# Four small SBUF tiles moved from ahead of the weight ring to behind it

## The reference

```python
mod = silu(c) @ w_ada + b_ada             # 2048 -> 6 * 2048: sh1, sc1, gt1, sh2, sc2, gt2
h = rms_norm(x, g_pre_mix) * (1 + sc1) + sh1
u_lru, u_gate, q, k, v, f = split(h @ w_in)          # 2048 -> 5 * 1024 + 8
y_lru = rg_lru(conv4(u_lru)) * gelu(u_gate)          # 16 blocks of 64, scan over the tokens
y_att = causal attention, 8 heads of 128, bias from cumsum(log_sigmoid(f + b_forget))
y = concat(rms_norm(y_lru), rms_norm(y_att)) @ w_out # 2048 -> 2048
x = x + gt1 * rms_norm(y, g_post_mix)
h = rms_norm(x, g_pre_mlp) * (1 + sc2) + sh2
y = square(relu(h @ w_ff1)) @ w_ff2                  # 2048 -> 8192 -> 2048
x = x + gt2 * rms_norm(y, g_post_mlp)
```

## Time and profile before

| | |
|---|---|
| median of 3 runs | 2133.91 us (2131.73 to 2133.93) |
| the profiled execution | 2131.73 us, of which its span, first to last instruction, is 2129.9 us |
| mean granted TensorE clock | 0.990 of full speed |
| TensorE busy | 2052.9 us, 96% of the span |
| VectorE, ScalarE, GpSimd busy | 1614.7, 797.4 and 99.2 us |
| HBM read and written | 313.20 and 10.52 MB |

### The profile page before, as it was taken

The page is one execution under the profiler, slowest core; times in us unless marked ns, Lnnn a source line. Parts: engine busy times, 40 slices in busy tenths (PEclk is TensorE's granted clock), DMA queues, the critical chain, the costliest instruction groups (busy, mean ns, idle before and its releaser), DMA issues.

```text
span 2129.9 us, 25152 instructions
## 1 busy us (share of the span) xinstructions
PE 2052.9 (96%) x9025; PEld 1673.3 (79%) x9025; DVE 1614.7 (76%) x1863; ACT 797.4 (37%) x1035; POOL 99.2 (5%) x105
## 2 busy tenths in 40 slices
PE   4999999999999999999999999999999999999997
PEld 4777778788778778888888888888888888888886
DVE  6998597876987887686776776876866867767766
ACT  5324622214553254343343343333333433433433
POOL 1001050000220001000000000000000000000000
PEclk8999999999999999999999999999999999999999
DMA  9995459856437862332332332333223323333334
GB/s 330 364 302 173 148 159 306 288 183 210 129 108 274 271 237 83 125 99 89 108 98 91 117 106 90 108 99 108 95 85 125 98 89 108 98 94 120 102 120 157
DMA packets 181582, 324.57 MB, mean 152 GB/s; under 512 B 12648, under 2 KB 49624, under 8 KB 179216
## 3 DMA queue, kind: packets, MB, share of 16 engines
q1 hardware_dynamic: 173600, 302.08, 43.9%
q0 software_dynamic: 3568, 16.95, 2.2%
q10 hardware_dynamic: 4352, 4.73, 0.7%
HBM read 313.20 MB, written 10.52 MB: 152 GB/s over the span
## 4 chain that ended last, share of the span: by engine, by line
PE 77%; DVE 14%; DMA 3%; issue 3%; ACT 3%; SPq 1%; DVEq 0%; ACTq 0%
PE pair L835 10%; PE pair L837 10%; PE pair L836 10%; PE pair L860 9%; PE pair L862 9%; PE pair L861 9%; PE bank L527 4%; PE bank L528 4%; PE bank L529 4%; DVE acc L1443 2%; DVE w_lo L1415 2%; PE bank L537 2%; PE bank L539 1%; PE bank L538 1%; DMA raw<-in_w_out_dram 1%
## 5 line engine op out<-in xcount | busy, mean ns | idle before, releaser
L1863 DVE TENSOR_TENSOR yg<-yg,pair 128x1024 f32<-128x1024 f32 x240 | 289.6, 1217 | 287.6 <-PE pair L862 287.5
L835 PE MATMUL pair<-h_hi,w_lo 128*128 128x512 f32 x1020 | 397.5, 390 | 0.0
L836 PE MATMUL pair<-h_lo,w_hi 128*128 128x512 f32 x1020 | 396.9, 389 | 0.0
L837 PE MATMUL pair<-h_hi,w_hi 128*128 128x512 f32 x1020 | 396.8, 389 | 0.0
L860 PE MATMUL pair<-w_hi,op_lo 128*128 128x512 f32 x840 | 329.9, 393 | 9.1 <-DVE op_lo L1830 8.6
L861 PE MATMUL pair<-w_lo,op_hi 128*128 128x512 f32 x840 | 327.2, 389 | 0.0
L862 PE MATMUL pair<-w_hi,op_hi 128*128 128x512 f32 x840 | 327.1, 389 | 0.0
L965 ACT ACTIVATE w_hi<-raw 128x1024 fp32r<-128x1024 f32 (+1 forms) x114 | 118.6, 1044 | 317.2 <-DMA raw<-in_w_in_dram 205.3
L835 PEld LDWEIGHTS pair<-h_hi,w_lo 128*128 128x128 f32 x1020 | 191.5, 188 | 39.9 <-issue 0.2
L836 PEld LDWEIGHTS pair<-h_lo,w_hi 128*128 128x128 f32 x1020 | 191.4, 188 | 39.9 <-issue 0.2
L837 PEld LDWEIGHTS pair<-h_hi,w_hi 128*128 128x128 f32 x1020 | 191.5, 188 | 39.9
(11 more groups left out here) (272 smaller groups left out, 2773.4 us busy)
## 6 DMA issues: line engine op xcount, KB each, us to landing
raw<-in_w_ada_dram SPq DMA_DIRECT2D x128, 512.0 KB, 4.7
w_raw<-in_w_ff_dram SPq DMA_DIRECT2D x128, 512.0 KB, 3.9
raw<-in_w_ff_dram SPq DMA_DIRECT2D x128, 512.0 KB, 4.6
raw<-in_w_in_dram SPq DMA_DIRECT2D x74, 512.0 KB, 4.8
gst<-in_w_ada_dram SPq DMA_DIRECT2D x64, 512.0 KB, 9.3
raw<-in_w_out_dram SPq DMA_DIRECT2D x32, 512.0 KB, 4.8
x_tok<-in_x_dram SPq DMA_DIRECT2D x4, 1024.0 KB, 8.6
xr<-in_x_dram POOLq DMA_DIRECT2D x4, 1024.0 KB, 7.8
```

Source lines behind the costliest of these rows:

```text
L835: pe.matmul(b, lo[:, cols], h_hi[:, kt, :], start=(kt == 0), stop=False)
L836: pe.matmul(b, hi[:, cols], h_lo[:, kt, :], start=False, stop=False)
L837: last = pe.matmul(b, hi[:, cols], h_hi[:, kt, :], start=False, stop=(kt == KT - 1))
L1863: dve.tensor_tensor(y, y, pairs[2 + (i + r) % 2][:, :, :], ALU.subtract if i == 6 else ALU.add).then_inc(product_read, 1)
```

## The change

The four tiles `bf`, `eps`, `mod` and `A1` are no longer allocated first. `A1` stands ahead of `S1`, and the other three behind `wf_raw`, as the last of the tiles that live through the whole kernel. No instruction, wait, DMA, loop or shape is changed.

```diff
-        bf = sb("bf", [HEADS, 1])
-        eps = sb("eps", [P, 1])
-        mod = sb("mod", [P, 4])
-        A1 = sb("A1", [P, KT])
         raw = sb("raw", [P, RING, 2 * COLS])
         w_hi = sb("w_hi", [P, RING, 2 * COLS], F32R)
         w_lo = sb("w_lo", [P, RING, 2 * COLS], F32R)
...
         cc = sb("cc", [P, 4, KT])
-        S1, A2, S2 = (sb(n, [P, KT]) for n in ("S1", "A2", "S2"))
+        A1, S1, A2, S2 = (sb(n, [P, KT]) for n in ("A1", "S1", "A2", "S2"))
         stat = sb("stat", [P, 96])
         lam = sb("lam", [P, 8, CT])
         wf_raw = sb("wf_raw", [P, KT, HEADS])
+        bf = sb("bf", [HEADS, 1])
+        eps = sb("eps", [P, 1])
+        mod = sb("mod", [P, 4])
```

## The result

The changed kernel takes 2169.35 us (median of 4 runs, 2168.16 to 2171.3), the kernel before 2133.8 us in the same session. The ratio is 1.0167, with a 95% interval of 1.0154 to 1.0178: it is slower by 35.6 us. The forecast was 2133.9 us with a range up to 2162.0. The result is outside the range and on the side that had a chance of 0.32.

The account below looks back on a forecast made before the run. The prediction took TensorE to bound the kernel (96% busy). It added 0 for every term to the profiled 2131.7 us, giving 2133.9 us as a median, with a range of 2111 to 2162 us.

Parts of the forecast that it names:

- What bounds the kernel: Whole kernel: TensorE busy 96% of the span, 77% of the chain; matmul cost changes come out almost one to one.
- VectorE, ScalarE, the moved tiles: 0: Operations on shifted tiles and few short uses of the four moved ones: 0, bound 2.4 us either way.
- DMA: 0, with 6.6 us either way: Loads written into raw, 43.7 us of the chain: 0, bounded by a 15% landing difference, 6.6 us.
- The rule on 256-byte boundaries: DMA writes into raw: 2048 bytes would need 68 beats instead of 65, some 2 us; left out of the sum.
- TensorE, the ring as streamed operand: 0: 3864 matmuls streaming the weight tiles, no cover, about 3500 counting fully: 0 taken, -35 to +23 us possible.
- one piece of 64 bytes: Streamed matmuls: one more 64-byte piece per misplaced run, 16 cycles or 6.7 ns each, 23 us either way.
- TensorE, the ring as stationary operand: 0, covered: 4608 matmuls loading the weight tiles: 0, since up to 39 ns more per load hides behind the matmul streaming beside it.
- The sum: Whole kernel: profiled 2131.7 us plus 0 for every term gives 2131.7, or 2133.9 us as a median.
- (b): Start distance in product and w1_piece: weight tiles and activations out of step, slower, 2157 or 2188 us; chance 0.28.
- (a): Matmuls streaming the weight tiles: faster from a multiple of 64, 2111 to 2099 us; chance 0.18.
- (c): Loads of raw slower or faster by up to 6.6 us, 2127 to 2140.5; chances 0.03 small, 0.02 faster, 0.04 slower.
- The 16-byte lines: SBUF lines of 16 bytes: all starts before and after are multiples of 32, so nothing would change.

Follow-up runs that it names:

- m2_fine: Layer left out, TensorE alone: float32r at fine distances, plain float32, bfloat16 and 256 columns; float32r of 512 columns settles between 226.7 and 240.0 ns.
- e1: Kernel before with one more 32-byte tile at the front, so weight tiles and activations both move up by 32: 2131.77 us, ratio 0.9999.
- m1_map: Also called the map: layer left out, TensorE alone, float32r matmuls at 256 pairs of start addresses plus finer ones; 226.7 ns at distance 0, 233.8 at 160.
- m3_order: Layer left out, TensorE alone: float32r with shorter weight blocks and mixed distances; one load in three off by 160 gives 233.1 ns each.

## Why the prediction was wrong, by its own steps

**What bounds the kernel.** Right. TensorE sets the time, and all of the loss is in TensorE's busy time. "Comes out one to one" was too strong; see the sum below.

**VectorE, ScalarE, the moved tiles: 0.** Right: 1221 and 1054 ns before and after.

**DMA: 0, with 6.6 us either way.** Right: landings of 4.5 and 3.8 us after 4.6 and 3.9, and e3 moved `raw` alone for nothing (0.9997). The difference between the two loads was indeed not the address. The rule on 256-byte boundaries of DMA: Bandwidth & Descriptors (the Trainium skill, How a descriptor splits into AXI transactions), cited in the prediction, would have shown as a longer landing of `raw` if it held for the written side; no lengthening is seen.

**TensorE, the ring as streamed operand: 0.** This is the step that failed. The term measured about +7 ns on each of the MLP's matmuls of this kind (227.1 to 234.0 over all starts, 226.7 to 233.3 in the round shown). The text itself said that the trace held no float32r matmul at another distance, and then settled on 0 because "everything else that I can compare in this trace is blind to the remainder". All that it compared ran at half the pace (L564, L729) or on other engines, and m2_fine shows that plain float32 gives the same 429 ns at all 17 distances tried. A row that cannot feel an effect is no evidence against it. The price set for the loss, one piece of 64 bytes or 6.7 ns, was near the truth by chance: the spacing is some 560 cycles instead of 544 at these distances, but about 551 at 64 bytes (229.7 ns) and 576 at 20 bytes (240.0), so no fixed piece of 64 bytes stands behind it.

**TensorE, the ring as stationary operand: 0, covered.** Failed too. The step asked whether the load would get longer, and it did not (188 ns). What it missed is that the place from which the block is loaded, against that of the streamed tile, lengthens the streaming, so that the 39 ns of cover are of no use. In the MLP these matmuls too went to 234.0 ns (from 226.7), and in the projection to 234.2 (from 227.3).

**The sum.** By the durations 4608 x 7 + 3864 x 6.7 ns = 58 us of added TensorE work. Rival (b) had "on both kinds some 8100 x 6.7 ns = 54", added in full: 2188 us. The trace shows where the rest went. Starts of the first matmul of a stage, before and after: the gates of the LRU (L633) 182.4 and 182.5; v (L537) 448.8 and 453.3; the MLP (L835) 789.1 and 798.0; its second product (L860) 835.1 and 845.2; the last of that loop (L862) 2071.8 and 2110.2. The first 182 us absorb everything; the likely reason, not tested, is that this stage is also bound by VectorE and DMAs. By the start of the MLP 8.9 us have come out, and the MLP adds 29.5. Windows of one round of the loop each, before and after:

```profile
930.84:1013.58 82.74, 82.06 (x362) 67.41 (x361) 60.21 (x58) 30.26 (x33) 0.00 (x0) 1.00 0.33 102
```

```profile
1014.91:1099.49 84.58, 84.40 (x362) 67.61 (x361) 60.22 (x57) 30.25 (x33) 0.00 (x0) 1.00 0.31 99
```

TensorE's work in a round grows by 2.34 us, its waiting shrinks from 0.68 to 0.18 us, and the round grows by 1.84 us. A slower TensorE waits less for VectorE: over the whole page the idle time ahead of the first matmul of the second product, which waits for `op_lo` from VectorE, falls from 9.1 to 2.3 us.

**The rivals.** (a), faster from a multiple of 64, is refuted by e1 and the map. (b) was the right mechanism, named with its place and even with "the two read streams of TensorE", and had 0.28; its form on both kinds got the 0.1 that the range left out. The prediction's own remark, that before all operands had the same remainder and after they did not, deserved more weight than the even spread that it got. (c) is refuted by e3.

**The 16-byte lines** of SBUF — State Buffer (the Trainium skill, Specifications), by which nothing would change, since all starts are multiples of 32: the measurement decides against it, for the same multiples of 32 give 226.7 to 234.5 ns. TensorE: Matmul & The Clock Gate (the Trainium skill, Step-by-step: what each phase is for) says that TensorE has two read ports and that loading the next weights does not take bandwidth from the running matmul. That agrees with bfloat16 and plain float32 here (no difference at 17 distances) and not with float32r, where the start of the streamed operand against that of the load shifts the spacing by up to 13 ns.

**What stays open.** Shown are the dependence on the distance modulo 256 for starts at multiples of 32, the one type of the three tried that feels it, and the loss and its return in the kernel. Not shown is what the two reads share, or that it is the reads that meet: the runs vary start addresses and see spacings. Nor is it shown why three spacings are long for one odd load, why equal starts at 4, 16 or 48 bytes are slower than equal starts at multiples of 32, and why blocks of fewer columns are no faster. Many group means lie near 544, 560 and 576 cycles (226.7, 233.3 and 240.0 ns), but single spacings of 230, 231 and 236 ns stand beside them, so no size of a wait can be read from them.

## What to carry to other kernels

In a kernel bound by float32r matmuls, the distance between the start of the stationary and that of the streamed tile is a tuning value. For matmuls of 512 columns keep all starts at multiples of 32 and the distance a multiple of 256 bytes for all operands of a stream, and treat every small tile allocated between them as part of it. For another number of columns measure first: at 256 columns a distance of 0 or 256 was among the slowest tried (119.7 ns, against 113.3 at 192). Here 160 bytes of bookkeeping tiles were worth 35.6 us of 2134, and 96 bytes of padding bring them back. When the trace holds no row at the new value of something, look for the rows that could feel it; rows of a slower type or another engine bound nothing.

## What the runs showed of the hardware that was not expected

Float32r at 512 columns takes 226.7 ns (544 cycles at 2.4 GHz) from start to start at best and up to 240.0 ns (576) at the worst distance, such as 20, 132 or 196 bytes (m2_fine). Bfloat16 takes 216 and plain float32 429 ns a pass at every distance tried (multiples of 32, m2_fine). For starts at multiples of 32 the pattern depends on the distance alone and repeats every 256 bytes; it needs no other engine (m1_map). With starts at 4, 16 or 48 bytes a distance of 0 no longer gives 226.7 ns but 231 to 238 (m1_map). The best distance depends on the number of columns: at 256 columns a distance of 192 gives 113.3 ns and a distance of 0 gives 119.7 (m2_fine), while at 512 columns 0 is best. One weight load in twelve that is off by 160 bytes lengthens three spacings in a row, and one in three lengthens all of them (m3_order).
